# Seven half-matrix products for eight in the MLP up projections of a two-layer trunk, with the low parts shared between two engines

## What is computed

```python
D_MODEL = 1024; SEQ = 512; DEPTH = 2; D_FF = 4 * D_MODEL

def squared_relu_mlp(h, w_up, w_down):
    return jnp.square(jax.nn.relu(h @ w_up)) @ w_down

for layer in range(DEPTH):
    hn = rmsnorm(h, mix_norm[layer])
    h = h + mixer(layer, hn)          # even_mixer or odd_mixer, ends in "@ w_out"
    h = h + squared_relu_mlp(rmsnorm(h, mlp_norm[layer]), w_up[layer], w_down[layer])
return rmsnorm(h, final_norm)
```

## Time and profile before

| | us |
|---|---|
| median of 3 runs (lowest to highest) | 1340.57 (1340.44 to 1342.28) |
| span of the profiled execution | 1338.8 |
| PE busy | 1298.3 |
| POOL busy | 658.7 |
| DVE busy | 567.6 |
| ACT busy | 535.5 |

### The profile page before, as it was taken

One profiled execution on the slowest core, in us unless ns is written; L12 is line 12 of the kernel. 1 busy time (PEld: TensorE's weight loads), 2 busy tenths in 40 slices (PEclk: granted clock), 3 DMA queues, 4 the chain that ended last, 5 costly groups with the idle time before them and its releaser, 6 DMA issues.

```text
span 1338.8 us, 18262 instructions
## 1 busy us (share of the span) xinstructions
PE 1298.3 (97%) x6685; PEld 1041.4 (78%) x6685; DVE 567.6 (42%) x913; ACT 535.5 (40%) x880; POOL 658.7 (49%) x809
## 2 busy tenths in 40 slices
...
DMA packets 198036, 108.87 MB, mean 81 GB/s; under 512 B 4570, under 2 KB 195280, under 8 KB 197968
## 3 DMA queue, kind: packets, MB, share of 16 engines
...
...
q0 software_dynamic: 416, 0.07, 0.0%
...
## 4 chain that ended last, share of the span: by engine, by line
PE 89%; DVE 6%; issue 2%; ACT 2%; DMA 1%; SPq 0%; DVEq 0%; ACTq 0%
PE ps L907 24%; PE ps L909 24%; PE ps L908 24%; PE ps L894 3%; PE ps L1318 1%; PE ps L957 1%; DVE arena L2362 1%; PE ps L958 1%; PE ps L959 1%; PE ps L1106 1%; PE ps L1392 1%; DMA rwkv_raw<-in_x 1%; PE ps L1075 1%; PE ps L1088 0%; PE ps L1382 0%
## 5 line engine op out<-in xcount | busy, mean ns | idle before, releaser
L811 POOL TENSOR_TENSOR w_lo<-raw_w,w_hi 128x256 fp32r<-128x256 f32 x760 | 617.3, 843 | 572.3 <-ACT w_hi L1471 572.3
L1471 ACT ACTIVATE w_hi<-raw_w 128x1024 fp32r<-128x1024 f32 x190 | 201.1, 1058 | 531.3 <-PE ps L909 422.8
L907 PE MATMUL ps<-hn_hi,w_hi 128*128 128x512 f32 x880 | 357.3, 406 | 0.3 <-DVEq L2085 0.3
L908 PE MATMUL ps<-hn_lo,w_hi 128*128 128x512 f32 x880 | 349.5, 397 | 0.0
L909 PE MATMUL ps<-hn_hi,w_lo 128*128 128x512 f32 x880 | 349.5, 397 | 0.0
L907 PE MATMUL ps<-hid_hi,w_hi 128*128 128x512 f32 x576 | 227.6, 395 | 0.0
L909 PE MATMUL ps<-hid_hi,w_lo 128*128 128x512 f32 x576 | 227.5, 395 | 0.0
L908 PE MATMUL ps<-hid_lo,w_hi 128*128 128x512 f32 x576 | 227.5, 395 | 0.0
L907 PEld LDWEIGHTS ps<-hn_hi,w_hi 128*128 128x128 f32 x880 | 166.4, 189 | 44.4 <-issue 4.2
L908 PEld LDWEIGHTS ps<-hn_lo,w_hi 128*128 128x128 f32 x880 | 166.5, 189 | 41.9 <-issue 2.9
L909 PEld LDWEIGHTS ps<-hn_hi,w_lo 128*128 128x128 f32 x880 | 166.2, 189 | 40.8
...
## 6 DMA issues: line engine op xcount, KB each, us to landing
raw_w<-in_w_up SPq DMA_DIRECT2D x64, 512.0 KB, 4.0
raw_w<-in_w_down SPq DMA_DIRECT2D x64, 512.0 KB, 4.0
raw_w<-in_o_w_in SPq DMA_DIRECT2D x27, 512.0 KB, 3.8
raw_w<-in_e_w_in SPq DMA_DIRECT2D x19, 512.0 KB, 3.8
raw_w<-in_e_w_out SPq DMA_DIRECT2D x8, 512.0 KB, 3.4
raw_w<-in_o_w_out SPq DMA_DIRECT2D x8, 512.0 KB, 3.7
rwkv_raw<-in_x SPq DMA_DIRECT2D x4, 512.0 KB, 7.3
...
```

Source lines behind the costliest of these rows:

```text
L811: nc.gpsimd.tensor_tensor(w_lo[:, n % CUT, ks], raw_w[:, n % RING, ks], w_hi[:, n % CUT, ks].bitcast(F32), ALU.subtract).then_inc(w_cut, 1)
L907: mm(o, a_hi, b_hi, start=(k == 0), stop=False)
L908: mm(o, a_hi, b_lo, start=False, stop=False)
L1471: A(w_hi[:, n % CUT], raw_w[:, n % RING], ACT.Copy).then_inc(w_high, 1)
```

## The change

The up projection of a pass (1024 features to 1024 hidden columns) is done in two halves p of 512 hidden columns, each as a 2 x 2 block product by Winograd's scheme with **seven products for eight**. The weight quarters are A and B (first 256 columns of the half, even and odd k tiles) and C and E (second 256 columns, even and odd); the activations are cut by even and odd k tile and by halves of 256 tokens. A unit is one product: four k steps x two column tiles x three matmuls, that is 24 of 256 columns. So a pass has 14 up units and, as before, 8 down units of 24 matmuls of 512 columns; the 22 units all go through four cut buffers (two new ones, `wx_hi` and `wx_lo`, beside the old). Loops become written-out code.

- **Weights.** Quarters load into eight places (A and B in the ring, C and E in `y_t`); the down slots of the pass take the same places as they come free. POOL makes t1 = A + C and t3 = C + E, DVE t2 = t1 + E and t4 = t2 + B, in place, each one instruction of 1024.
- **Low parts.** POOL makes those of units 1 to 4 and from 13 on in four parts of 256, DVE those of 5 to 12 (`u` 4 to 11) in one of 1024. ACT makes all 22 high parts.
- **Results.** Three pairs of banks hold X, Z and V. m6 is added onto m1, m7 onto m6, m3 onto m5, in the bank; ahead of that ACT copies m1, m5 and m6 out (`copied`), and m7 behind it. m4 takes m2's bank and waits for quarter c11. The quarters c11, c12, c22, c21 are then each a DVE pass from PSUM and a relu pass in SBUF, followed as before by square and high part on ACT and low part on DVE. Down units use banks 6 and 7; the first takes its k steps in the order `DOWN_K`.
- **Activations.** `project_out` also copies each gained tile, and for each pair of tiles DVE makes four differences of 256 tokens, ACT their high parts and DVE their low parts (`part`, `part_high_of`, `part_low_of`).
- **Norm.** PE takes its norm product behind the second up unit of the first pass, DVE the reciprocal behind its sum t2 of that pass.
- Layer 1's first loads and cuts, and the final norm's writes to `y_mix`, wait for the last units of the MLP.

The diff, cut to its core (12 columns of indentation taken off); in this order the tables, SP, POOL, PE, ACT and DVE:

```diff
+UP = [("m1", 0), ("m1", 1), ("m2", 0), ("m2", 1), ("m5", 0), ("m6", 0), ("m3", 0), ("m7", 0), ("m4", 0),
+      ("m5", 1), ("m6", 1), ("m3", 1), ("m7", 1), ("m4", 1)]
...
+READS = {"m1": "A", "m2": "B", "m5": "A", "m6": "A", "m3": "E", "m7": "C", "m4": "A"}
...
+X_BANK, Z_BANK, V_BANK, D_BANK = 0, 2, 4, 6
+BANK_OF = {"m1": X_BANK, "m6": X_BANK, "m7": X_BANK, "m5": Z_BANK, "m3": Z_BANK, "m2": V_BANK, "m4": V_BANK}
+COPIES = [("m1", 0), ("m5", 0), ("m1", 1), ("m6", 0), ("m7", 0), ("m5", 1), ("m6", 1), ("m7", 1)]
+QUARTERS = [("c11", 0), ("c11", 1), ("c12", 0), ("c22", 0), ("c21", 0), ("c12", 1), ("c22", 1), ("c21", 1)]
+LOWS = [("c11", 0), ("c11", 1), ("c12", 0), ("c22", 0), ("c21", 0), ("c12", 1), ("c22", 1), ("c21", 1)]
...
+DOWN_K = [0, 1, 2, 3, 6, 7, 4, 5]
...
+def cut_on_pool(layer, i, u):
+    return u >= NUP - 2 or u < 4
...
+    for i in range(4):
+        for p in range(2):
+            unit_cut(sp, layer, i, U["m2", p])
+            sum_made(dve_sum, DVE_SUMS, i, ("t4", p))
+            load_down(4 * p, i)
+            unit_cut(sp, layer, i, U["m3", p])
+            sum_made(dve_sum, DVE_SUMS, i, ("t2", p))
+            sum_made(pool_sum, POOL_SUMS, i, ("t3", p))
+            load_down(4 * p + 1, i)
+            unit_cut(sp, layer, i, U["m7", p])
+            load_down(4 * p + 2, i)
+            unit_cut(sp, layer, i, U["m4", p])
+            load_down(4 * p + 3, i)
+        if i < 3:
+            for j in range(KT):
+                unit_cut(sp, layer, i, NUP + j)
+                load_up(DOWN_AT[j], i + 1)
...
+    def low_unit(i, u):
...
+        for q in range(PARTS):
+            c = slice(q * 256, (q + 1) * 256)
+            nc.gpsimd.tensor_tensor(lo_[:, c], raw_[:, c], hi_[:, c].bitcast(F32), ALU.subtract
+                                    ).then_inc(u_cut_pool, 1)
...
+    def sum_third(i, p):
...
+        low_unit(i, 1)
+        sum_first(i, 0)
+        low_unit(i, 2)
+        low_unit(i, 3)
+        sum_third(i, 0)
+        sum_first(i, 1)
+        sum_third(i, 1)
+        for u in range(NUP - 2, UNITS):
+            low_unit(i, u)
...
+    def up_unit(i, u):
...
+            pe.wait_ge(quartered, len(QUARTERS) * (4 * layer + i))
+        if q in copied_first:
+            pe.wait_ge(copied, turn_of(COPIES, layer, i, (copied_first[q], p)))
+        if q == "m4":
+            pe.wait_ge(quartered, turn_of(QUARTERS, layer, i, ("c11", p)))
...
+            x_hi, x_lo = moving[q](k)
+            for m in range(2):
+                om = o[:, m * HT:(m + 1) * HT]
+                a_hi, a_lo = hi_[:, k, m * P:(m + 1) * P], lo_[:, k, m * P:(m + 1) * P]
+                opens = q in ("m1", "m2", "m5", "m4") and k == 0 and m == 0
+                mm(om, a_hi, x_hi, start=opens, stop=False, skip_group_check=True)
+                mm(om, a_hi, x_lo, start=False, stop=False, skip_group_check=True)
+                ins = mm(om, a_lo, x_hi, start=False, stop=(k == 3), skip_group_check=True)
+        ins.then_inc(u_done, 1)
+    def down_unit(i, j):
...
+        if j >= 2:
+            pe.wait_ge(added, KT * n + j - 1)
+        elif n:
+            pe.wait_ge(added, KT * n)
...
+                half = int(k >= 4)
+                for c in (("c11", "c21") if k % 4 < 2 else ("c12", "c22")):
+                    pe.wait_ge(hid_ready, turn_of(LOWS, layer, i, (c, half)))
+            mm(o, hi_[:, k, :], hid_hi[:, k, :], start=(at == 0), stop=False)
+            mm(o, hi_[:, k, :], hid_lo[:, k, :], start=False, stop=False)
+            ins = mm(o, lo_[:, k, :], hid_hi[:, k, :], start=False, stop=(at == KT - 1))
...
+def part_high_of(layer, pair):
...
+    act.wait_ge(parted, 4 * layer + pair + 1)
+    A(hn_hi[:, 2 * pair, HT:T], d_parts[:, 0, :], ACT.Copy)
+    A(d_hi[:, :, pair, :], d_parts[:, 1:4, :], ACT.Copy).then_inc(part_high, 1)
...
+    def copy(i, q, p):
+        dst, waits = {"m1": (relu_t[:, 0, :], "c11"), "m6": (relu_t[:, 1, :], "c12"),
+                      "m5": (spare[:, 1, :], "c22"), "m7": (spare[:, 0, :], "c21")}[q]
+        n = 4 * layer + i
+        unit_done(act, layer, i, U[q, p])
+        if p:
+            act.wait_ge(hid_ready, turn_of(LOWS, layer, i, (waits, 0)))
+        elif n:
+            act.wait_ge(hid_ready, turn_of(LOWS, layer, i, (waits, 1)) - len(LOWS))
+        A(dst, ps[:, BANK_OF[q] + p, :], ACT.Copy).then_inc(copied, 1)
...
+    for i in range(4):
+        n = 4 * layer + i
+        if i == 0:
+            act.wait_ge(summed, KT * (2 * layer + 1))
+        copy(i, "m1", 0)
+        high_unit(layer, i, 4)
+        high_unit(layer, i, 5)
+        if i == 0:
+            norm(2 * layer + 1)
+        high_unit(layer, i, 6)
+        hidden(i, "c11", 0)
+        high_unit(layer, i, 7)
+        copy(i, "m5", 0)
+        copy(i, "m1", 1)
+        high_unit(layer, i, 8)
+        copy(i, "m6", 0)
+        high_unit(layer, i, 9)
+        hidden(i, "c11", 1)
+        high_unit(layer, i, 10)
+        hidden(i, "c12", 0)
+        copy(i, "m7", 0)
+        high_unit(layer, i, 11)
+        hidden(i, "c22", 0)
+        high_unit(layer, i, 12)
+        hidden(i, "c21", 0)
+        copy(i, "m5", 1)
+        high_unit(layer, i, 13)
+        copy(i, "m6", 1)
+        high_unit(layer, i, 14)
+        high_unit(layer, i, 15)
+        hidden(i, "c12", 1)
+        copy(i, "m7", 1)
+        high_unit(layer, i, 16)
+        hidden(i, "c22", 1)
+        high_unit(layer, i, 17)
+        hidden(i, "c21", 1)
+        if i < 3:
+            for u in range(18, 22):
+                high_unit(layer, i, u)
...
+def part(layer, pair):
...
+    odd = flat[:, HT:].rearrange("p (a t) -> p a t", t=HT)[:, 0:3:2, :]
+    link(V.tensor_tensor(d_parts[:, 0:2, :], flat[:, 0:T].rearrange("p (a t) -> p a t", t=HT), odd,
+                         ALU.subtract))
+    link(V.tensor_tensor(d_parts[:, 2, :], d_parts[:, 1, :], flat[:, 0:HT], ALU.subtract))
+    V.tensor_tensor(d_parts[:, 3, :], flat[:, T:T + HT], d_parts[:, 2, :], ALU.add).then_inc(parted, 1)
+def part_low_of(layer, pair):
...
+    V.tensor_tensor(hn_lo[:, 2 * pair, HT:T], d_parts[:, 0, :], hn_hi[:, 2 * pair, HT:T].bitcast(F32),
+                    ALU.subtract)
+    V.tensor_tensor(d_lo[:, :, pair, :], d_parts[:, 1:4, :], d_hi[:, :, pair, :].bitcast(F32),
+                    ALU.subtract).then_inc(part_low, 1)
...
+    def low_unit(i, u):
+        g = unit(layer, i, u)
+        dve.wait_ge(u_high, g + 1)
+        hi_, lo_ = cut_buffers(layer, g)
+        V.tensor_tensor(lo_, place(layer, place_of(layer, u)), hi_.bitcast(F32), ALU.subtract
+                        ).then_inc(u_cut_dve, 1)
...
+    def quarter_of(i, c, p):
...
+        unit_done(dve, layer, i, U[last, p])
+        dve.wait_ge(copied, turn_of(COPIES, layer, i, (copy_of, p)))
+        if c == "c12":
+            ins = V.tensor_tensor(flat, z, flat, ALU.subtract)
+        elif c == "c22":
+            ins = V.tensor_tensor(flat, flat, x, ALU.subtract)
+        else:
+            ins = V.tensor_tensor(flat, v, flat, ALU.add)
+        ins.then_inc(quartered, 1)
+        dve.wait_ge(quartered, turn_of(QUARTERS, layer, i, (c, p)))
+        rms_half = rms_t[:, 0:HT] if c in ("c11", "c12") else rms_t[:, HT:T]
+        V.scalar_tensor_tensor(out=t, in0=t, scalar=0.0, in1=over(rms_half, 1, 2), op0=ALU.max, op1=ALU.mult
+                               ).then_inc(relued, 1)
...
+    for i in range(4):
+        low_unit(i, 4)
+        sum_second(i, 0)
+        if i == 0:
+            norm(2 * layer + 1)
+        low_unit(i, 5)
+        quarter_of(i, "c11", 0)
+        sum_fourth(i, 0)
+        low_unit(i, 6)
+        low_hidden(i, "c11", 0)
+        low_unit(i, 7)
+        quarter_of(i, "c11", 1)
+        low_unit(i, 8)
+        low_unit(i, 9)
+        sum_second(i, 1)
+        low_hidden(i, "c11", 1)
+        quarter_of(i, "c12", 0)
+        low_unit(i, 10)
+        sum_fourth(i, 1)
+        quarter_of(i, "c22", 0)
+        low_hidden(i, "c12", 0)
+        low_unit(i, 11)
+        low_hidden(i, "c22", 0)
+        quarter_of(i, "c21", 0)
+        low_hidden(i, "c21", 0)
+        quarter_of(i, "c12", 1)
+        quarter_of(i, "c22", 1)
+        low_hidden(i, "c12", 1)
+        quarter_of(i, "c21", 1)
+        low_hidden(i, "c22", 1)
+        low_hidden(i, "c21", 1)
+        for j in range(KT):
             add(i, j)
```

More of the change, by code:

```diff
@@ L411, in make_plan @@
         put("norm", 2 * layer + 1, bank=NBANK - 1)
-        for j in range(8):
-            put("mlp", layer, j, bank=j, times=8)
     put("norm", 4, bank=3)
@@ L1528, in project_out @@
-                    high_gained("mlp_norm", 8 * layer + k)
+                    if k in (5, 6):
+                        high_unit(layer, 0, k - 5)
+                    if k == 7:
+                        full(act, "out", layer, 6)
+                        act.wait_ge(w_cut, PARTS * (n0 - 1))
+                        high_unit(layer, 0, 2)
+                    drained(act, "out", layer, k)
+                    j = 8 * layer + k
+                    gain = col_a("mlp_norm", j)
```

(17 more changed lines are left out.)

348 lines of the change are left out of this document (239 added, 109 removed).

## The result

| | us |
|---|---|
| before, median of 4 runs | 1341.4 |
| after, median of 4 runs (lowest to highest) | 1388.6 (1385.3 to 1390.9) |
| ratio (95% interval) | 1.0352 (1.0331 to 1.0374) |
| span of the profiled execution, before and after | 1338.8 and 1384.9 |

A forecast was written before the change was run, and what follows sets the result against it. PE, busy 97% of the span, was taken as the bound; the span of 1338.8 plus 9 for later passes and 17 for first passes gave 1364.8, with 1.8 outside the trace 1366 us; range 1326 to 1388.

The forecast's parts named there:

- the first pass of each layer: DVE's extra work behind the last output tile and the reciprocal make each first pass 8.5 us longer, two layers 17.
- a part overlap: In the first passes, part of the 8.5 us added to each was said to overlap; no size given.
- A later pass: Steady pass, 1.9 us longer by the sum, or about 0.9 with cheaper POOL sums; taken as 1.5, six passes 9 us.
- the two prices: PE's 256-column matmul in up units: 0.117 us if in proportion to columns, 0.127 with an extra per instruction; 0.127 taken.
- a turn: First down unit waits for the low part of second-half quarter c21: PE waits 0.7 us (0 to 1.5).
- The place and the mechanism: At index 11 PE waits 3.3 us for ACT's copy of m5, behind quarter c21, which waits for DVE.
- the blocking: Time POOL's operations hold up DVE before index 11 of a pass: at most 7.7 us, taken as 6.
- My sign of being wrong: Wrong if later passes' up phases are under 44 us, or DVE's 1024-wide operations stay near 1.22.
- Rows 8 and 10: Earlier trace rows read as DVE and POOL, each reading two SBUF operands, taking turns by whole instructions; up to 512 wide.
- Rival 1: POOL's sums fall in DVE's pauses, so PE sets the pace: 1330 us, chance 25%.
- Rival 4: PE's clock falls in waits of 3 to 5 us; each pass loses 2.5, eight 20: 1386 us, chance 5%.
- Covered at no cost: Weight loads, ACT's work, POOL's 49 us a pass and written-out loops were said to add no time.

The follow-up runs named there:

- e12: Last kernel with all reorderings, turn and first-pass edits, plus POOL's four sums and the second to fourth pairs' differences on 4 columns: 1311.2 us, ratio 0.9768.
- e1: The changed kernel with POOL's four sums of a pass made on 4 columns of 1024: 1345.1 us, ratio 1.0043 to before.
- e4: The changed kernel with DVE's reciprocal behind the low part of unit 6 in each layer's first pass: 1382.7 us, ratio 1.0339 to before.
- e7: The changed kernel with the differences of the second to fourth pair of tiles made on 4 columns instead of 256: 1378.4 us, ratio 1.0271 to before.
- e3: The changed kernel with POOL's t3 of the first half and t1 of the second ahead of unit 4's low part: 1367.4 us, ratio 1.0207 to before.

## Why the prediction was wrong

The direction was right, but the time, 1388.6, lies above the forecast of 1366 and just above the range's end of 1388.

- **The step that failed: the first pass of each layer.** Its term was 17 us for two layers and measured 35.8. I put the first low part near 9 us and it came at 20.4. I counted what stands behind the last output tile as if DVE were free when that tile ends. It was 7.6 us behind (L2315 above): the differences of the earlier pairs, 2.9 for three operations and 4.1 for two low parts beside POOL, no longer fit between tiles. What I had put at 9 then took 12.8, with POOL's turns in it (L2307: 3.15, where the same operation takes 0.95 with POOL idle in e12). The sum also had no wait of PE at the norm's product, which is 6.3 us in each layer, and no half clock, some 6 us in layer 0 by the estimate above. And I let "a part overlap". What single runs took from a first pass is 7.5 (sums, e1), 2 (reciprocal's place, e4) and 3 to 4 (differences, e7), some 13 of 18; the rest is not split, and the wait at index 6 is the largest place that the last trace still shows.
- **A later pass** came out near its size: six of them 9 us by the sum, 10.6 measured. That was luck, since its parts were less good and cancelled. A matmul takes 0.118 and not 0.127: of the two prices, the one in proportion to the columns was right, worth some 26 us more over eight passes than I counted. Against it stand waits at indexes 5 and 6 (1.6 us a pass), which I had not foreseen, though the second is for the same copy as at index 11, one half earlier; a turn of 1.9 where I took 0.7; and 1.6 of half clock in four passes, which I held to be a rival of its own.
- **The place and the mechanism** of the later passes were right. PE waits at index 11 for the copy behind quarter c21, for 2.7 us (3.3 by the sum). Index 11 starts 35.4 us into the pass, against 36.8 worked out; the blocking is 4.9 where I took 6. Of the 2.6 us that the cheaper matmul gained PE up to there (30.9 for 33.5), 1.2 went into waits, 4.5 in all. My sign of being wrong, up phases of later passes under 44 us, was drawn too tight: two of the six took 43.9 to 44.0, those at full clock behind the wait, and the mechanism is the same in them.
- **Rows 8 and 10 read as turns by whole instructions** held for 1024 columns: 1.22 becomes 3.0 to 3.4 beside sums of 2.41. The Trainium skill, "SBUF — State Buffer", section "SBUF: two separate sides", has this rule; the trace agrees, with 3.41 for 1.22 beside one sum.
- **Rival 1** (POOL's sums fall in DVE's pauses) was wrong of this kernel, but it is what the reordering in e3 makes partly true. **Rival 4** had the clock right in kind: it cost four later passes 1.6 us each and the first passes more, not 2.5 in all eight.
- The stretch up to the first MLP and the mixer of layer 1 changed by +2.7 and -2.8. I had named no such term, and its cause stays open.
- **Covered at no cost** held: PE shows no wait for a load in the MLP passes.
